# RWKV stage of a two-layer backbone: a new order of one body's work, a gather into two buffers, four spreads instead of eight, and y's stores on two queues

## The chip, the cores and the metric

The kernel runs on one core of a Trainium2 chip. The core has a matrix engine (TensorE, "PE" in the profile, its weight loads "PEld"), a vector engine (VectorE, "DVE"), a scalar engine (ScalarE, "ACT"), a general engine (GpSimd, "POOL") and SyncE ("SP"), which here only issues DMAs. Each engine runs its own list of instructions in order, and the engines meet through semaphores. The metric is the device time of one execution in microseconds, the median of the runs; lower is better.

## The reference

Two layers over a latent stream of 2048 tokens and a context of 256 tokens, width 1024. The first layer mixes with multi-head latent attention and a Fourier transform. The second is a bidirectional RWKV-7 time mix. Only its scan matters here:

```python
def step(s, inp):
    w_t, k_t, v_t, kk_t, a_t = inp[:5]
    sa = jnp.einsum('bhvk,bhk->bhv', s, kk_t)
    s = (s * w_t[:, :, None, :]
         - sa[..., None] * (kk_t * a_t)[:, :, None, :]
         + v_t[..., None] * k_t[:, :, None, :])
    y = jnp.einsum('bhvk,bhk->bhv', s, inp[5]) if len(inp) > 5 else None
    return s, y
```

There are 16 heads of width 64 and two directions; the state of a head is 64 x 64 and runs over all 2304 tokens. Both directions' y are added, normalised by head, gated and projected. Everything is float32.

## The kernel before

Stages follow each other: modulation, the first layer's projections, attention, Fourier mixing, merge, the second layer's input projection (`project1`), the scan (`rwkv`, L1663), and the last merge (`merge1`, L2433). The change touches only `rwkv`.

**Tiling.** Heads are worked in pairs (a pair fills 128 partitions), tokens in groups of 256, a group in 4 chunks of 64. 8 pairs times 9 groups give 72 bodies, each with both directions (d = 0 forward, d = 1 backward). The loop over bodies is unrolled (`bodies`, L1764).

**A chunk as matrices.** Inside a chunk the recurrence becomes a triangular system. For a chunk: products of keys with queries are made (`scores`, matmul L1972) and masked (`masks`, L2357) into tiles NB (removal) and KK (new keys). The 64 x 64 triangular part of NB is inverted: its 16 x 16 diagonal blocks on GpSimd (`invert`), the parts off the diagonal by three rounds of matmuls (`far_p` L1988, `first_order` L1998, `second_w` L2007, `higher_orders` L2017), whose sums VectorE adds (`add_orders`, rw_XT, L2376).

**The way of the blocks.** SP stores NB's blocks to `scratch_products` (`keep_products`, L1808), fetches the diagonal blocks into g_in and g_at (`gather`, L1816), GpSimd inverts them, SP stores g_out (`keep_inverses`, L1823) and fetches them spread over XB (`spread`, eight DMAs, L1834).

**The serial part.** For each chunk c of body n: `step_values` (L2026), `step_begin` (the read of the state S: L2036, and the start of the update and of y: L2043 to L2050), ScalarE copies r1 (`take_r1`, L2206), `step_sa` (L2062, needs XT), ScalarE copies sa (`take_sa`, L2210), `step_end` (L2070 into S's bank, L2075 into y's), VectorE writes the state (`carry`, L2349), ScalarE copies y (`take_y`, L2220). `step_begin` of the next chunk reads S, and after that read waits for `take_y`, since y's bank is written again. I call the four carries of a body c0 to c3.

**Work ahead.** Each body also does pieces for later bodies: m = n+1 (far blocks), k = n+3 (turns: transposes of K, B, V through TensorE, L1953, with four copies on ScalarE, L2196; scores, masks, the bonus L1936 and L2340), l = n+4 (low-rank L1928, rates L2163, decays L2177, keys, queries L2325, weights L2334 and L2335). Loads (L1780, L1781) are for n+5. The order of all this on each engine is written out by hand in a function `body(n, has)` for each engine; `has` drops the parts that fall off either end. y of the body before is stored by ScalarE in two pairs of DMAs (`store_y`, L2226).

A PSUM bank is shared by several of these: bank 5 holds scores of direction 0 and the bonus, bank 3 scores of direction 1 and the turned V, bank 4 the turned K and B in turn.

## Time and profile before

| | us |
|---|---|
| median of 3 runs (5325.24 to 5332.35) | 5329.45 |
| profiled execution | 5343.89 |
| its span, first to last instruction | 5341.9 |

| engine | busy us | share of the span | instructions |
|---|---|---|---|
| PE | 4732.2 | 89% | 50126 |
| DVE | 2522.5 | 47% | 4088 |
| ACT | 1828.2 | 34% | 4367 |
| POOL | 1306.7 | 24% | 2817 |

The span's shares mix stages with different limits: the RWKV stage is the part from about 3,600 to 5,060 us. A busy matmul engine is a modelled figure, since matmuls overlap. Rows give the engine, the line, the operation and tiles as out<-in; the bracket at a row's end is how long the engine stood idle before it, and who ended that.

### The profile page before, as it was taken

The page shows a single profiled execution, that of the slowest core. Times are in us where ns is not written, and L with a number is a line of the kernel's source. Part 1 is how long each engine was busy: PE and PEld are TensorE (multiplying, and loading weights), DVE is VectorE, ACT ScalarE, POOL GpSimd, SP SyncE. Part 2 cuts the span into 40 slices and gives each one's busy share as a digit, 9 for nine tenths or more (in the row PEclk, how much of TensorE's full clock was granted, in tenths as well). Part 3 has the DMA queues.
Part 4 walks back from the last instruction along what each step waited for, and adds up shares of the span by engine and source line. Part 5 has one row for each costly group of instructions (what it writes and reads, how often), then busy time and mean ns, then how long its engine had stood idle before and what let it go on. Part 6 is the DMA issues. An engine that isn't in the chain of part 4 may idle for free. (4 is left out here: it accounts for less than half of the span.)

```text
span 5341.9 us, 125176 instructions
## 1 busy us (share of the span) xinstructions
PE 4732.2 (89%) x50126; PEld 2658.0 (50%) x50126; DVE 2522.5 (47%) x4088; ACT 1828.2 (34%) x4367; POOL 1306.7 (24%) x2817
## 2 busy tenths in 40 slices
PE   5999996999999997898999999967888888888689
PEld 2666663333333333444444444436666666666544
DVE  1334433666666662222222222235666666666476
ACT  1221221443343431132211212125555555555322
POOL 0111111222222220000000000005655565565333
PEclk7999997999999998999999999989999999999899
DMA  7221211000000006432211112135666666666475
GB/s 290 61 64 62 70 61 63 4 23 24 23 23 22 23 6 245 163 137 60 73 59 59 59 59 71 55 90 133 149 151 142 145 149 138 150 147 144 106 267 172
DMA packets 928982, 526.66 MB, mean 99 GB/s; under 512 B 661344, under 2 KB 879072, under 8 KB 921440
## 3 DMA queue, kind: packets, MB, share of 16 engines
q1 hardware_dynamic: 850144, 500.73, 32.7%
q10 hardware_dynamic: 78336, 18.89, 1.7%
q8 instruction: 357, 5.85, 0.5%
q14 instruction: 145, 1.19, 0.1%
HBM read 330.98 MB, written 188.49 MB: 97 GB/s over the span
## 5 line engine op out<-in xcount | busy, mean ns | idle before, releaser
L1565 PE MATMUL p_bU<-keep_hT,p_slab 128*128 128x512 f32 (+1 forms) x2592 | 1029.5, 559 | 12.9 <-DMA p_slab<-in_o_w_in_dram 7.5
L1565 PEld LDWEIGHTS p_bU<-keep_hT,p_slab 128*128 128x128 f32 x2592 | 493.3, 191 | 544.1 <-issue 512.3
L914 PE MATMUL at_bS<-at_qT,at_kT 97*64 97x512 f32 (+1 forms) x2368 | 602.5, 598 | 6.7 <-issue 6.1
L1046 DVE TENSOR_REDUCE at_mx<-at_bM 128x1 f32<-128x512 f32 (+1 forms) x656 | 400.5, 629 | 355.3 <-PE at_bM L880 352.4
L1009 ACT ACTIVATE at_pT<-at_bS 128x512 f32<-128x512 f32 (+1 forms) x592 | 346.9, 591 | 461.4 <-PE at_bS L914 382.4
L1637 DVE SCALAR_TENSOR_TENSOR p_z<-p_u,p_shift,p_z 128x2306 f32<-128x2306 f32 x26 | 68.2, 2622 | 770.3 <-ACT p_z L1595 770.3
L1892 POOL TENSOR_TENSOR rw_g_at<-rw_g_at,rw_g_prod 64x14 f32<-64x14 f32 (+6 forms) x1008 | 318.0, 315 | 79.0
L1890 POOL TENSOR_TENSOR rw_g_prod<-rw_g_at 64x14 f32<-64x14 f32 (+6 forms) x1008 | 314.2, 312 | 79.1
L2349 DVE TENSOR_TENSOR rw_S<-rw_bank,rw_dec 128x128 f32<-128x128 f32 x288 | 84.1, 292 | 474.2 <-PE rw_bank L2070 474.2
L933 PE MATMUL at_bO<-at_pT,at_va 128*64 128x512 f32 x1152 | 300.3, 599 | 0.0
L837 POOL TENSOR_TENSOR at_sum_pool<-at_sum_pool,at_pT 128x512 f32<-128x512 f32 x128 | 192.8, 1506 | 433.3 <-ACT at_pT L1009 421.9
L914 PEld LDWEIGHTS at_bS<-at_qT,at_kT 97*64 97x64 f32 x2368 | 161.1, 138 | 266.2 <-issue 214.0
L1589 ACT COPY p_u<-p_bU 128x512 f32<-128x512 f32 (+1 forms) x130 | 69.7, 542 | 643.6 <-PE p_bU L1565 630.0
L1067 DVE TENSOR_TENSOR at_sum_vector<-at_sum_vector,at_pT 128x512 f32<-128x512 f32 x320 | 276.2, 863 | 13.1 <-ACT at_pT L1009 9.7
L1903 POOL MEMSET rw_zeros<- 128x1040 f32 x1 | 1.0, 964 | 1105.0 <-POOLq L2685 1105.0
L1355 PE MATMUL m_bY<-m_w,m_mT 128*128 128x512 f32 x576 | 251.8, 595 | 0.0
L453 PE MATMUL p_bG<-keep_w_in,p_hT 128*128 128x512 f32 x576 | 250.1, 592 | 0.0
L880 PE MATMUL at_bM<-at_kTb,at_qTb 96*64 96x512 bf16 (+1 forms) x1312 | 224.4, 365 | 12.0 <-DVE at_mx L1046 10.9
L2576 PE MATMUL m_bY<-m_w,m_oT 128*128 128x512 f32 x512 | 225.3, 599 | 1.5 <-DVE m_oT L2646 1.5
L2043 PE MATMUL rw_bank<-rw_Vt,rw_Kt 64*64 64x64 f32 x2304 | 183.8, 228 | 27.9 <-ACT rw_ysb L2220 19.5
L2062 PE MATMUL rw_bank<-rw_r,rw_XT 64*64 64x64 f32 x2304 | 133.3, 233 | 79.8 <-DVE rw_XT L2376 74.8
L1972 PE MATMUL rw_bank<-rw_AR,rw_Kc 64*64 64x128 f32 x2304 | 168.1, 279 | 37.4 <-issue 30.1
(263 smaller groups left out, 9401.7 us busy)
## 6 DMA issues: line engine op xcount, KB each, us to landing
rw_zin<-scratch_heads SPq DMA_DIRECT2D x144, 512.0 KB, 4.9
rw_XB<-scratch_inverses SPq DMA_DIRECT2D x576, 64.0 KB
mod_w<-in_ada_w_dram SPq DMA_DIRECT2D x6, 4096.0 KB, 23.6
scratch_heads<-p_z SPq DMA_DIRECT2D x24, 1024.0 KB, 4.9
rw_lin<-scratch_lora SPq DMA_DIRECT2D x144, 128.0 KB, 5.5
scratch_bv<-rw_bv SPq DMA_DIRECT2D x144, 128.0 KB, 2.3
scratch_products<-rw_NB SPq DMA_DIRECT2D x288, 64.0 KB, 3.9
scratch_y<-rw_ysb ACTq DMA_DIRECT2D x288, 64.0 KB, 2.8
```

What stands on the lines that cost most here:

```text
L453: last = pe.matmul(bG[:, j, :], hT[:, s, k, :], w_in[:, k, E_G0 + 512 * j:E_G0 + 512 * (j + 1)], start=(k == 0), stop=(k == KD - 1))
L880: last = pe.matmul(bM[rows, (FIRST_ITEM[b] + i) % 2, 0:n], qTb[:, s, q0 + VH * x:q0 + VH * x + VH], kTb[:, s, c:c + n], start=True, stop=True)
L914: last = pe.matmul(bS[rows, g % 3, 0:nq * P], kT[:, s, k * P + VH * x:k * P + VH * x + VH], qT[:, s, q0 * P:(q0 + nq) * P], start=True, st ...
L933: last = pe.matmul(out[rows, 0:nq * P], va[:, s, 2 * pair + x, :], pT[:, (g + x) % SLOTS, 0:nq * P], start=(pair == 0), stop=(pair == nk / ...
L1009: nc.scalar.activation(pT[:, g % SLOTS, 0:n], bS[:, g % 3, 0:n], ACT.Exp, scale=SCALE).then_inc(exp_done, 1)
L1046: nc.vector.tensor_reduce(mx[:, j, piece:piece + 1], bM[:, (FIRST_ITEM[b] + i) % 2, 0:n], AX.X, ALU.max).then_inc(max_red, 1)
L1067: nc.vector.tensor_tensor(acc, acc, tile, ALU.add).then_inc(added[False], 1)
L1355: last = pe.matmul(bY[:, j, :], mT[:, s, k, :], w[:, k, j * 512:(j + 1) * 512], start=(k == 0), stop=(k == KD - 1))
L1565: last = pe.matmul(bU[:, n % 4, 0:w], slab[:, i, k, :], hT[:, k, tok:tok + w], start=(k == 0), stop=(k == KD - 1))
L1890: link(nc.gpsimd.tensor_tensor(prod, N[:, k + 1:, k:k + 1].broadcast_to([2 * half, rows, k]), N[:, k:k + 1, 0:k].broadcast_to([2 * half, r ...
L1892: link(nc.gpsimd.tensor_tensor(below, below, prod, ALU.add))
L2576: last = pe.matmul(bY[:, 2 * s + j, :], oT[:, s, k, :], w[:, k, j * 512:(j + 1) * 512], start=(k == 0), stop=(k == KD - 1))
```

## The change

Bodies compute the same. Parts:

- Blocks: g_in and g_at get two buffers each, and both receive all 64 diagonal blocks. The layout in the scratch tensors is changed so that each spread fetches both directions at once, four DMAs in place of eight; `crossed` and `laid` keep the books. `gather` waits for the inversion two bodies back, no longer for the last one.
- GpSimd: two turned copies at the start instead of one reversed, and two copies out over 64 partitions instead of four over 32.
- SP's order in a body: y's store of direction 1, spread, products, bonus store, loads, gather, inverses. Before: bonus store, loads, products, inverses, gather, spread.
- TensorE: scores of direction 0 come right behind the first step's begin; the bonus and the turns of V and B come behind chunk 1's begin; the scores of L1972 against Kc for direction 1 move to chunk 3.
- ScalarE: y's store of direction 0 behind the copy of sa; the copies of turned tiles move one or two chunks later, half of the turned K into the next body.
- VectorE: queries behind carry 2, the bonus product behind carry 1, its queries for k = n+3 behind carry 0.

```diff
-        g_in, g_at = (core.sb(n, [2 * BLOCKS, SUB * SUB]) for n in ("g_in", "g_at"))
+        g_in, g_at = (core.sb(n, [2 * BLOCKS, 2, SUB * SUB]) for n in ("g_in", "g_at"))
...
                 def gather(m):
                     sp.wait_ge(n_st, 16 * 4 * (m.n + 1))
-                    if m.since(1):
-                        sp.wait_ge(inv_done, 4 * m.n)
-                    for d in range(2):
-                        sp.dma_start(by_block((g_in, g_at)[d], d), diagonal("products")[BLOCKS * d:BLOCKS * (d + 1)]).then_inc(g_l, 16)
+                    if m.since(2):
+                        sp.wait_ge(inv_done, 2 * m.n - 2)
+                    for tile in (g_in, g_at):
+                        sp.dma_start(by_block(tile[:, m.two]), diagonal("products")).then_inc(g_l, 16)
...
-                    for turned in (1, 0):
-                        for d in range(2):
-                            for h, (rows, other) in enumerate(ACROSS):
-                                sp.dma_start(XB[rows if turned else other, m.two, turned, d], whole("inverses", d, h, turned)).then_inc(xb_l, 16)
+                    for order in range(2):
+                        for half, (rows, _) in enumerate(HEADS2):
+                            sp.dma_start(XB[rows, m.two, order].rearrange("p d c t -> p (d c) t"), delivered(order, half)).then_inc(xb_l, 16)
...
                 def body(n, has):                        # SP
+                    if has[0] and n.since(1):
+                        store_y(n.on(-1), 1)
+                    if has[1]:
+                        spread(n.on(1))
                     if has[3]:
+                        keep_products(n.on(3))
                         store_bonus(n.on(3))
                     if has[5] and n.since(-3):
                         load(n.on(5))
                     if has[3]:
-                        keep_products(n.on(3))
+                        gather(n.on(3))
                     if has[2]:
                         keep_inverses(n.on(2))
-                    if has[3]:
-                        gather(n.on(3))
-                    if has[2]:
-                        spread(n.on(2))
...
                 def body(n, has):                        # TensorE, first half
-                    if has[3]:
-                        bonus(k)
                     if has[0]:
                         step_values(n, 0, lambda i: higher_orders(n, 0, (2 * i, 2 * i + 1)))
                         step_begin(n, 0, lambda i: higher_orders(n, 1, (2 * i, 2 * i + 1)))
                     if has[3]:
-                        turn(k, 2)
+                        scores_free(k, 0, 0)
+                        scores(k, 0, 0, range(NCH))
...
+                    if has[3]:
+                        bonus(k)
                     if has[0]:
                         step_sa(n, 1)
                     if has[3]:
-                        scores(k, 0, 1, (2, 3))
+                        turn(k, 2)
                     if has[0]:
                         step_end(n, 1)
+                    if has[3]:
+                        turn(k, 1)
...
                 def body(n, has):                        # ScalarE
                     if has[0]:
                         take_r1(n, 0)
+                    if has[2]:
+                        for e in range(2):
+                            turned(j, 0, 1, e)
+                    if has[0]:
+                        take_sa(n, 0)
                         if n.since(1):
                             store_y(n.on(-1), 0)
                     if has[3]:
-                        for h in range(2):
-                            for e in range(2):
-                                turned(k, 2, h, e)
                         decay_of_chunks(k)
-                    if has[0]:
-                        take_sa(n, 0)
...
                     if has[0]:
                         take_y(n, 0)
                         take_r1(n, 1)
-                        if n.since(1):
-                            store_y(n.on(-1), 1)
```

ScalarE around a body's first step, before (rw_r is r1, rw_ee the rates, rw_Vt the turned V):

```order
L2206 COPY rw_r<-rw_bank 128x128
L2226 DMA scratch_y<-rw_ysb 64x4x64 x2
L2196 COPY rw_Vt<-rw_bank 64x4x64 x4
L2185 COPY rw_dec<-rw_ep 128x4
L2186 COPY rw_dec<-rw_ep 128x4
L2210 COPY rw_sa<-rw_bank 128x128
L2163 ACTIVATE rw_ee<-rw_bank,rw_par 128x256 x2
L2220 COPY rw_ysb<-rw_bank 128x2x64
L2206 COPY rw_r<-rw_bank 128x128
```

The same place after, from the end of one body into the next:

```order
L2210 COPY rw_Kt<-rw_bank 64x4x64 x2
L2220 COPY rw_r<-rw_bank 128x128
L2210 COPY rw_Kt<-rw_bank 64x4x64 x2
L2224 COPY rw_sa<-rw_bank 128x128
L2240 DMA scratch_y<-rw_ysb 64x4x64 x2
L2199 COPY rw_dec<-rw_ep 128x4
L2200 COPY rw_dec<-rw_ep 128x4
L2177 ACTIVATE rw_ee<-rw_bank,rw_par 128x256 x2
L2234 COPY rw_ysb<-rw_bank 128x2x64
L2220 COPY rw_r<-rw_bank 128x128
```

The copy of sa moved ahead of the store of y, the decay copies stay behind the store, and the copy of y (rw_ysb) now has the store in front of it.

VectorE from the last carry of a body to the first of the next, before:

```order
L2349 TENSOR_TENSOR rw_S<-rw_bank,rw_dec 128x128
L2334 TENSOR_TENSOR rw_Kc<-rw_kd,rw_en 128x512
L2335 SCALAR_TENSOR_TENSOR rw_Bc<-rw_b,rw_en 128x512
L2325 TENSOR_TENSOR rw_AR<-rw_ep,rw_zin 128x8x64
L2326 TENSOR_TENSOR rw_AR<-rw_ep,rw_zin 128x8x64
L2340 TENSOR_TENSOR rw_bv<-rw_bank,rw_zin 128x512
L2376 TENSOR_TENSOR rw_XT<-rw_bank,rw_XT 128x256 x2
L2349 TENSOR_TENSOR rw_S<-rw_bank,rw_dec 128x128
```

And after:

```order
L2366 TENSOR_TENSOR rw_S<-rw_bank,rw_dec 128x128
L2351 TENSOR_TENSOR rw_Kc<-rw_kd,rw_en 128x512
L2352 SCALAR_TENSOR_TENSOR rw_Bc<-rw_b,rw_en 128x512
L2393 TENSOR_TENSOR rw_XT<-rw_bank,rw_XT 128x256 x2
L2374 TENSOR_TENSOR rw_NB<-rw_bank,rw_tri 128x512
L2366 TENSOR_TENSOR rw_S<-rw_bank,rw_dec 128x128
```

Three operations left the stretch ahead of rw_XT, and one mask came in behind it.

SP over one body, before, from the bonus store:

```order
L1789 DMA scratch_bv<-rw_bv 128x256 x2
L1780 DMA rw_zin<-scratch_heads 128x4x256
L1781 DMA rw_lin<-scratch_lora 64x2x256
L1780 DMA rw_zin<-scratch_heads 128x4x256
L1781 DMA rw_lin<-scratch_lora 64x2x256
L1808 DMA scratch_products<-rw_NB 64x4x64 x4
L1823 DMA scratch_inverses<-rw_g_out 128x16x16
L1816 DMA rw_g_in<-scratch_products 32x16x16
L1816 DMA rw_g_at<-scratch_products 32x16x16
L1834 DMA rw_XB<-scratch_inverses 64x4x64 x8
```

And after, from the store of y:

```order
L1851 DMA scratch_y<-rw_ysb 64x4x64 x2
L1845 DMA rw_XB<-scratch_inverses 64x8x64 x4
L1820 DMA scratch_products<-rw_NB 64x4x64 x4
L1797 DMA scratch_bv<-rw_bv 128x256 x2
L1788 DMA rw_zin<-scratch_heads 128x4x256
L1789 DMA rw_lin<-scratch_lora 64x2x256
L1788 DMA rw_zin<-scratch_heads 128x4x256
L1789 DMA rw_lin<-scratch_lora 64x2x256
L1828 DMA rw_g_in<-scratch_products 64x16x16
L1828 DMA rw_g_at<-scratch_products 64x16x16
L1835 DMA scratch_inverses<-rw_g_out 128x16x16
```

Products moved ahead of the bonus store and the loads; the gather moved behind the loads and has twice the rows; the spread stands at the body's start.

## Rows read from the trace of the kernel before

**Rows 1.** One stretch: busy us of PE, PEld, DVE, ACT, POOL; clock, DMA share, GB/s.

```profile
4000.00:4400.00 400.00, 326.62 (x10226) 269.51 (x10223) 252.39 (x504) 234.36 (x703) 230.53 (x686) 0.97 0.64 146
```

**Rows 2.** The carry's line: duration ns min/median/max, first and last start us.

```profile
L2349 DVE TENSOR_TENSOR rw_S<-rw_bank,rw_dec x288: 291/292/293, 3638.4 to 5055.2; 128x128 f32<-128x128 f32 x144
```

**Rows 3.** Timeline: carries of one body and TensorE's issue wait (start us, us).

```profile
4235.97 0.29 DVE L2349 TENSOR_TENSOR rw_S<-rw_bank,rw_dec 128x128 f32<-128x128 f32 x1 [2.09 <-PE rw_bank L2070]
...
4239.71 0.29 DVE L2349 TENSOR_TENSOR rw_S<-rw_bank,rw_dec 128x128 f32<-128x128 f32 x1 [0.99 <-PE rw_bank L2070]
...
4243.14 0.29 DVE L2349 TENSOR_TENSOR rw_S<-rw_bank,rw_dec 128x128 f32<-128x128 f32 x1 [0.61 <-PE rw_bank L2070]
...
4244.21 0.45 PE L1998 MATMUL rw_bank<-rw_XB,rw_Pm 64*64 64x64 f32 x8 [0.61 <-issue]
...
4247.63 0.29 DVE L2349 TENSOR_TENSOR rw_S<-rw_bank,rw_dec 128x128 f32<-128x128 f32 x1 [1.08 <-PE rw_bank L2070]
...
4253.85 0.29 DVE L2349 TENSOR_TENSOR rw_S<-rw_bank,rw_dec 128x128 f32<-128x128 f32 x1 [2.05 <-PE rw_bank L2070]
```

**Rows 4.** Waits of TensorE, 3,800 to 4,880 us: total us, times, longest.

```profile
PE rw_bank L2062 <- DVE rw_XT L2376: 56.4, 52, 1.3
PE rw_bank L2070 <- ACT rw_sa L2210: 37.6, 68, 1.8
PE rw_bank L1998 <- issue: 23.7, 13, 3.3
PE rw_bank L2043 <- ACT rw_ysb L2220: 12.8, 23, 0.6
```

**Rows 5.** Timeline of VectorE, from a body's c3 to the next c0.

```profile
4208.45 0.29 DVE L2349 TENSOR_TENSOR rw_S<-rw_bank,rw_dec 128x128 f32<-128x128 f32 x1 [1.04 <-PE rw_bank L2070]
...
4209.86 0.69 DVE L2325 TENSOR_TENSOR rw_AR<-rw_ep,rw_zin 128x512 f32<-128x512 f32 x1
...
4211.88 0.74 DVE L2376 TENSOR_TENSOR rw_XT<-rw_bank,rw_XT 128x256 f32<-128x256 f32 x2
```

**Rows 6.** Timeline of TensorE, the same stretch.

```profile
4208.32 1.12 PE L1936 MATMUL rw_bank<-rw_q,rw_same 128*128 128x512 f32 x2
...
4210.94 0.66 PE L1953 MATMUL rw_bank<-keep_ident,rw_zin 128*128 128x128 f32 x4
4212.76 0.45 PE L2062 MATMUL rw_bank<-rw_r,rw_XT 64*64 64x64 f32 x8 [1.17 <-DVE rw_XT L2376]
4213.01 1.09 PE L1928 MATMUL rw_bank<-rw_lin,rw_wl 64*64 64x256 f32 x16
4214.32 0.27 PE L2070 MATMUL rw_bank<-rw_sa,rw_Bt 64*64 64x64 f32 x2 [0.21 <-ACT rw_sa L2210]
```

**Rows 7.** Timeline of ScalarE; ACTq is its DMA issue.

```profile
4210.22 1.84 ACTq L2226 DMA_DIRECT2D scratch_y<-rw_ysb  x2
4212.15 1.50 ACT L2196 COPY rw_Vt<-rw_bank 64x256 f32<-64x256 f32 x4 [1.67 <-PE rw_bank L1953]
...
4214.16 0.85 ACT L2163 ACTIVATE rw_ee<-rw_bank,rw_par 128x256 f32<-128x256 f32 x2
...
4216.11 1.27 ACTq L2226 DMA_DIRECT2D scratch_y<-rw_ysb  x2
```

**Rows 8.** SP: issues of one body, and its longest wait in 54 bodies.

```profile
4208.48 5.59 SPq L1834 DMA_DIRECT2D rw_XB<-scratch_inverses  x8
...
SPq L1816 <- DMA scratch_products<-rw_NB: 82.9, 51, 3.3
```

**Rows 9.** Waits of GpSimd, the same 54 bodies.

```profile
POOL rw_g_at L1884 <- DMA rw_g_at<-scratch_products: 310.6, 54, 9.7
```

**Rows 10.** DMA: busy tenths (40 slices) from 4,217.4 to 4,223.4; then packets 4,209.4 to 4,229.4.

```profile
DMA  6689999999999798999899999999999999987653
...
DMA packets 9474, 2.96 MB, mean 148 GB/s; under 512 B 7934, under 2 KB 9470, under 8 KB 9470
...
q8 instruction: 4, 0.07, 1.4%
```

More of the change, by code:

```diff
@@ L1742, in rwkv, with crossed, laid @@
         ACROSS = [(HEADS2[h][0], HEADS2[1 - h][0]) for h in range(2)]
+        def crossed(h, d):
+            return h if d == 0 else 1 - h
+        def laid(turned, d):
+            return 1 - turned if d == 0 else turned
         def pos(d, c):
@@ L1987, in far_p @@
                         for rows, other in ACROSS:
-                            last = pe.matmul(bank[INV_AT[d]][other, C * c:C * c + C], NB_[rows, m.kept, d, c, 0, :], XB[rows, m.two, 1, d, c, :],
+                            last = pe.matmul(bank[INV_AT[d]][other, C * c:C * c + C], NB_[rows, m.kept, d, c, 0, :], XB[rows, m.two, laid(1, d), d, c, :],
                                              start=(c == 0), stop=True, skip_group_check=True)
@@ L1997, in first_order @@
                         for rows, _ in HEADS2:
-                            last = pe.matmul(bank[INV_AT[d]][rows, GT + C * c:GT + C * c + C], Pm[rows, d, c, :], XB[rows, m.two, 0, d, c, :],
+                            last = pe.matmul(bank[INV_AT[d]][rows, GT + C * c:GT + C * c + C], Pm[rows, d, c, :], XB[rows, m.two, laid(0, d), d, c, :],
                                              start=(c == 0), stop=True, skip_group_check=True)
@@ L2141, in body @@
                         step_values(n, 3)
-                        step_begin(n, 3)
+                    if has[3]:
+                        scores_free(k, 1, 1)
+                        scores(k, 1, 1, (0, 1))
+                    if has[0]:
+                        step_begin(n, 3, (lambda i: scores(k, 1, 1, (2 + i,))) if has[3] else None)
+                    elif has[3]:
+                        scores(k, 1, 1, (2, 3))
                     if has[3]:
@@ L2262, in body @@
                     if has[3]:
-                        turned(k, 1, 0, 1)
+                        turned(k, 2, 0, 1)
+                        for e in range(2):
+                            turned(k, 2, 1, e)
                     if has[0]:
                         take_sa(n, 2)
-                    if has[3]:
-                        for e in range(2):
-                            turned(k, 1, 1, e)
                     if has[4]:
@@ L2272, in body @@
                         take_y(n, 2)
+                    if has[3]:
+                        turned(k, 1, 0, 0)
+                    if has[0]:
                         take_r1(n, 3)
+                    if has[3]:
+                        turned(k, 1, 0, 1)
+                        for e in range(2):
+                            turned(k, 1, 1, e)
+                    if has[0]:
                         take_sa(n, 3)
@@ L2374, in add_orders @@
                     grown = XT[:, m.two, d].rearrange("p c t -> p (c t)")
-                    less = grown if which else XB[:, m.two, 0, d].rearrange("p c t -> p (c t)")
+                    less = grown if which else XB[:, m.two, laid(0, d), d].rearrange("p c t -> p (c t)")
                     nc.vector.tensor_tensor(grown, bank[INV_AT[d]][:, XT_COLS], less, ALU.add).then_inc(xt_out[d], 1)
@@ L2389, in body @@
                     link = Link(v, dch, EL * l.n)
-                    if has[3]:
-                        bonus(k)
                     if has[0]:
```

144 lines of the change are left out of this document (69 added, 75 removed).

## The prediction, made before the changed kernel ran

> **What bounds the kernel now.** I read the busy times by stretch first. The RWKV stage runs from about 3,600 us to 5,055 us, and in it no engine is full: in 400 us TensorE is busy 327, VectorE 252, ScalarE 234, GpSimd 231, the DMA engines 64%, at a granted clock of 0.97 of the full 2.4 GHz [rows 1]. So the stage is bound by the order in which engines wait for each other. Its clock is the carry of the state, four times a body: 288 carries from 3638.4 to 5055.2 us, thus 1416.8 / 71.75 = 19.75 us a body [rows 2]. Next I read single carries, to know a body when little disturbs it. c0 to c0 takes 3.74 + 3.43 + 4.49 + 6.22 = 17.88 us in one body [rows 3]; the average body is 1.87 us longer. The waits of TensorE, over 54 bodies, name two kinds of loss [rows 4]. One is order: 56.4 us for rw_XT (1.04 a body), 37.6 for rw_sa (0.70), 12.8 for rw_ysb. The other is called "issue": the sequencer waits for nothing that the profile shows. The largest issue group has 23.7 us in 13 waits, the longest 3.3 us. I read these as code that arrives late: four packets of a queue of kind "instruction" land in 20 us, 0.07 MB together, while loads of the next body fill the DMA engines for over 5 us on end [rows 10].
>
> The inversion on GpSimd does not bound it. It sits idle 310.6 us in 54 bodies, 5.75 a body, for its gathered blocks [rows 9], so a loop of 14 us of work has room in 19.75.
>
> **The change, part by part.** Times of one body, c3 at 4208.45 us.
>
> *From c3 to c0.* Before, the bonus matmul (1.12 us, until 9.44) stood ahead of the new body's first work [rows 6], and the values' matmuls (0.25) ahead of the read of S, near 9.7. It goes; the read can start when the carry is written (8.45 + 0.29 and a hand-over), so about 0.9 earlier. Then VectorE: Kc, Bc, two AR from 9.86, bv, then XT at 11.88, done at 12.62; TensorE waited 1.17 us for it and began the sa matmul at 12.76 [rows 5, 6]. After, only Kc and Bc stand ahead of XT, to 9.86, and the matmuls that XT adds up, which end where the turn begins (10.94), end 0.9 earlier, so XT is ready near 10.75. In the place of the turn of V (4 records in 0.66 us) stand all scores of one direction, 16 records of 128 columns. Bound below by half of the low-rank's 16 records of 256 columns (1.09 / 2 = 0.55), above by 1.09; I take 0.8, nearer to the middle because records have a start that does not halve. sa then starts at 10.9, low-rank takes 1.09 behind it, and the update of the state starts at 12.25 instead of 14.32. ScalarE hides: its copy of sa no longer stands behind y's store, four turned copies (1.50 us) and two of the decay, only behind two turned copies. Gain 2.05 us.
>
> *From c0 to c1.* Here a new wait appears. ScalarE's store of y (two DMAs, 1.27 us in one place and 1.84 in the other, during which it does nothing else [rows 7]) moves behind the copy of sa, together with the decay copies (0.3) and two rates (0.85), and only then comes the copy of y (0.27), which frees the bank that TensorE writes next. sa's copy ends at about 11.7; 11.7 + 1.27 + 0.3 + 0.85 + 0.27 = 14.4, while TensorE comes at 13.4 (carry at 12.8, its read 0.35 later, 0.2 of matmuls). So 1.0 us of waiting (1.6 if the store takes 1.84). Queued behind it: the rest of the step, the bonus matmul (1.06 more here), sa, the turn of V, and by them the next carry. Rest 0.7, bonus 1.06, sa 0.25, its copy 0.55, carry 0.5 give c1 at 17.5, 4.7 after c0, against 3.73. Loss 0.95. The other store of y, on SP's queue now, costs ScalarE nothing; that saves a second 1.27, which lay beside TensorE's work except for some 0.3 of waiting for sa.
>
> *From c1 to c2.* The turn of B comes ahead of the values and the far products behind the start of the step instead of in front. The same work stands in both, but the scores that filled TensorE's wait for the copy of sa are gone. Bounds: nothing, or 0.5 (a copy of 0.27 and two hand-overs). I take 0.2 loss.
>
> *From c2 to c3.* The turn of K must wait until ScalarE has copied all of the turned B. Three of those copies (1.50 for four [rows 7], so 1.1) now stand behind the copy of r1, beside which TensorE has only half a microsecond of the step left. Bounds: 0.6 later, if the copies hide behind a full step, to 1.3 with the 0.2 of scores in front of the step. The stretch in rows 3 (4.49) has an issue wait of 0.61 in it [rows 3], which a body without stalls has not, so against it the loss is between 0 and 0.7. I take 0.6, since the copies stand right behind r1.
>
> *SP's queue and GpSimd.* Eight spreads took 5.59 us to issue [rows 8]; four take 2.8, or 5.6 if twice the rows cost twice the issue; both fit ahead of the far products. SP waited 82.9 us in all for products to land before it could gather [rows 8]; now loads and bonus stores fill that time. All of this is hidden already: TensorE's waits have no group for rw_XB worth a term, so it earns 0. It must not become late, though. Products issued 3 us into the body land by 8 or so, the gather goes out behind the loads near 15, lands by 20, the inversion takes 14, its store 3, and the spread goes out at a body's start and lands some 5 us in; the far products ask for it near 9. That leaves 3 to 4 us. The gathered blocks are fetched twice (64 KB instead of 32 for each tile): 1,024 more packets in 9,474 a body [rows 10]. The inverter's four copies out of 32 partitions become two of 64: less work, on an idle engine, 0.
>
> The Trainium skill, "DMA: Bandwidth & Descriptors", section Specifications, asks for at least 512 B a descriptor, and the doubled gather moves 64 B pieces; by that it would be the dearest part. The trace has DMA engines 64% busy with most packets under 512 B already, so it decides little here.
>
> *Sum.* 17.88 - 2.05 + 0.95 + 0.2 + 0.6 = 17.6 us for a body without stalls. The order alone thus gives 0.3 against the quick body. The rest hangs on code stalls. Before, they and what hangs on them are 19.75 - 17.88 + 0.6 = 2.5 us a body. After, TensorE stands 1.0 and 1.0 us still at two new places in the quick half of a body, and code can arrive meanwhile. Bounds: none is absorbed (2.5) or both waits swallow their like (0.5). I take 1.5. Body: 19.1, or 0.6 to 0.65 less; times 72 is 43 to 47. The profiled execution took 5343.9 us with a span of 5341.9; the median of the runs is 5329.45, 14.4 less, and I take the gain from that: 5286.
>
> **Rivals.**
> *No gain.* Stalls only move: with 2.2 a body, 19.8 again, 5320 to 5339. For it: the stalls stand at several lines [rows 4], so their place hardly matters. Against it: the quick body lost only 0.6 to them, while single waits elsewhere reach 3.3 [rows 3, 4], so they depend on what runs beside them.
> *Slower.* Loads now go out behind the bonus store, and that behind c1: their saturated 5 to 8 us cover the far products, both last steps and the second-order matmuls, where TensorE runs through code fastest. Two of four code packets are then late instead of one. Price: stalls of 3.3 instead of 2.5, so 17.6 + 3.3 = 20.9 at worst, 20.6 at 3.0; 0.85 times 72 is 61: 5390. It decides from 2.2 of stalls a body. For it: saturation before began already at c1 [rows 10], and moving it later by 3 us keeps it in the quick half. Against it: products no longer stand behind the loads.
> *Large gain.* Nearly all stalls fall under the two waits: 17.6 + 0.8 = 18.4, 1.35 times 72 is 97: 5232.
> *Blocks late.* If the spread misses the far products, body length is set by GpSimd's 14 us plus a hand-over of 5, 19 us: the forecast's time by another way, so it needs no chance of its own.
>
> **How the numbers follow.** Forecast 0.50, no gain 0.14, slower 0.20, large gain 0.16. Two tenths of a percent is 10.7 us, about what a measurement of this kernel can tell from no change: below 5319 is faster, above 5340 slower. Faster 0.67 (forecast, large gain, a little of no gain), same 0.12, slower 0.21. The forecast's own range is 5262 to 5310; the whole range is 5222 to 5352.
>
> **What would show it.** TensorE's group of rw_XT under the sa matmul falls from 56.4 us to under 15; that of rw_ysb rises from 12.8 to over 40; a new group for the turn of K behind ScalarE's rw_Bt appears with 30 to 60; c3 to c0 falls to near 4.3 us, c0 to c1 rises to 4.7. Issue waits, all groups, fall by a third. GpSimd's wait stays 4 us a body or more. It is wrong if a group for rw_XB shows on TensorE, if low-rank waits for the loads, or if issue waits grow.

## The result: 0.6% slower, and where the time went

The changed kernel takes 5358.0 us (median of 5 runs, 5350.2 to 5368.6), the kernel before 5329.2 (5 runs, 5325.2 to 5332.4). The ratio is 1.0059, 95% interval 1.0046 to 1.0072. The forecast was 5286 us. The profiled execution took 5368.6 us with a span of 5366.8; before it was 5343.9 and 5341.9, so the two profiles differ by 25 us where the medians differ by 29.

The profile of before is thus of an execution 14.7 us above its median, or 0.2 us a body; where bodies of two profiles are compared below, a difference of that size can be chance.

First the same stretch of 400 us as [rows 1] (busy us of PE, PEld, DVE, ACT, POOL; clock, DMA share, GB/s):

```profile
4000.00:4400.00 400.00, 333.72 (x10114) 278.02 (x10106) 250.56 (x496) 223.16 (x694) 236.82 (x649) 0.98 0.70 147
```

TensorE ran fewer matmuls in it (10,114 for 10,226) and was busy longer; the DMA engines went from 64% to 70%. The carry's line answers to [rows 2]; duration in ns, then first and last start:

```profile
L2366 DVE TENSOR_TENSOR rw_S<-rw_bank,rw_dec x288: 258/292/293, 3640.6 to 5080.8; 128x128 f32<-128x128 f32 x144
```

(5080.8 - 3640.6) / 71.75 = 20.07 us a body, for 19.75 before: 0.33 more, times 72 is 24 us, the whole difference of the two profiles. So nothing outside of this stage is needed to explain it.

The timeline of VectorE gives one body, as [rows 3] do (start, us, and in brackets the idle time before and its releaser):

```profile
4319.97 0.29 DVE L2366 TENSOR_TENSOR rw_S<-rw_bank,rw_dec 128x128 f32<-128x128 f32 x1 [2.05 <-PE rw_bank L2087]
...
4323.31 0.71 DVE L2323 TENSOR_TENSOR_SCAN rw_cs<-rw_reset,rw_ee 128x256 f32<-128x256 f32 x1
4324.05 0.29 DVE L2366 TENSOR_TENSOR rw_S<-rw_bank,rw_dec 128x128 f32<-128x128 f32 x1
...
4328.38 0.75 DVE L2381 TENSOR_TENSOR rw_Pm<-rw_bank,rw_far 128x256 f32<-128x256 f32 x2
4329.04 0.28 DVE L2366 TENSOR_TENSOR rw_S<-rw_bank,rw_dec 128x128 f32<-128x128 f32 x1
...
4334.12 0.29 DVE L2366 TENSOR_TENSOR rw_S<-rw_bank,rw_dec 128x128 f32<-128x128 f32 x1 [2.04 <-PE rw_bank L2087]
...
4339.52 0.29 DVE L2366 TENSOR_TENSOR rw_S<-rw_bank,rw_dec 128x128 f32<-128x128 f32 x1 [1.31 <-PE rw_bank L2087]
```

c0 to c1 is 4.08, c1 to c2 4.99, c2 to c3 5.08, c3 to c0 5.40. The second and the third of these carries, c1 and c2, have no bracket: VectorE came to them straight from the instruction before. That is so at 66 of the 72 carries c1 and 69 of the 72 carries c2; before, it was so at none, and in [rows 3] all five had waited for TensorE. Only c2 pays for it. The last matmuls into S's bank ahead of these two carries:

```profile
4323.78 0.23 PE L2087 MATMUL rw_bank<-rw_sa,rw_Bt 64*64 64x64 f32 x2
...
4328.45 0.23 PE L2087 MATMUL rw_bank<-rw_sa,rw_Bt 64*64 64x64 f32 x2
```

c1 starts 0.04 us behind their end, c2 0.36. Over the stage the medians are 0.05 and 0.37 us after, 0.05 and 0.12 before.

The starts of all 288 carries, read from that timeline, give each of the four stretches over the stage (a quickest tenth is the tenth percentile of each stretch by itself):

```
us                       c0-c1   c1-c2   c2-c3   c3-c0   body
before, mean              3.96    4.59    4.99    6.23   19.75
after, mean               4.98    4.23    5.14    5.73   20.07
before, quickest tenth    3.73    3.43    4.08    5.97
after, quickest tenth     4.07    4.04    5.08    4.56
forecast, no stalls       4.68    3.63    5.09    4.17   17.6
```

The waits of TensorE, 3,820 to 4,900 us, hence 53.8 bodies, answer to [rows 4] (total us, times, longest):

```profile
PE rw_bank L1968 <- ACT rw_Bt L2210: 38.9, 51, 0.8
PE rw_bank L2060 <- ACT rw_ysb L2234: 32.0, 36, 2.1
PE rw_bank L2034 <- issue: 22.3, 12, 3.4
PE rw_bank L2087 <- ACT rw_sa L2224: 19.7, 53, 0.4
```

An "issue" wait is idle time of TensorE that nothing in the profile ends. The rw_XT group is gone; the turn of K waits for the turned B, and rw_ysb rose from 12.8 to 32.0, not to over 40. All groups of that view together, by the body: issue 1.62 before and 1.53 after, waits for engines or transfers 1.96 and 1.81. So the listed waits fell a little. What is left of a body, busy time and gaps too short for the view, grew from 16.17 to 16.73, more than the body itself. Issue waits did not fall by a third, but they moved. By the TensorE timeline of the whole stage 1.46 of 1.52 us a body stood between c1 and c3 before; now 1.15 of 1.42 stand between c3 and c0.

Issue waits above 0.3 us end some 2.8 us (tenth to ninetieth percentile 2.3 to 3.3, 84 waits) behind the start of a packet of 16 KB of the queue of kind "instruction"; before it was 2.5 us (2.3 to 2.8, 81 waits). There are four such packets a body in both kernels. That ties most of these waits to code that arrives late, and suggests that it came 0.3 us slower. It is a reading of times that go together; "late code" below means these waits.

The DMA engines show why it may. First 6 us around a c3 (4,312.3 to 4,318.3, c3 at 4314.26; 40 slices), then the queue SP issues to, over 3,820 to 4,900 us (packets, MB, share of 16 engines), in the kernel after:

```profile
DMA  9999977879999999999999999985646100158788
...
q1 hardware_dynamic: 506679, 146.86, 64.7%
```

and the same queue in the kernel before:

```profile
q1 hardware_dynamic: 435341, 139.39, 55.9%
```

In [rows 10] the full stretch lay from c1 (4218.6) to c2 (4222.0); now it ends behind c3. On average over the bodies, counting packets where they start (a value above 1 means that they run on into the next us):

```
us after c3          0    1    2    3 ...  10   11   12   13   14   15   16   17   18   19
DMA share before  0.29 0.32 0.36 0.71     0.95 0.99 0.96 0.94 0.80 0.70 0.64 0.54 0.42 0.28
DMA share after   0.84 0.82 0.62 0.60     0.61 0.47 0.43 0.52 0.50 0.71 0.83 0.90 1.04 1.13
64 B before        146   62    9    7        0    0    0   29  197  504  694  695  515  222
64 B after         555  892  765  566        0    0    0    0    0    0    0    3  187  514
```

Before, the 64 B packets (gathers and the inverses' store) ran behind the loads. Now there are 3,967 a body instead of 2,982, and they run into the loads: the trace's packets of 64 B take 13 ns of a DMA engine on average, for 10 before, which makes 3.12 us of all 16 engines a body for 1.92. The median is 11 ns in both, so a part of the packets take much longer.

Two issuing engines feel it too. ScalarE and SP, in their timelines (ACTq and SPq are DMA issues):

```profile
4613.39 2.34 ACTq L2240 DMA_DIRECT2D scratch_y<-rw_ysb  x2
4615.82 0.20 ACT L2199 COPY rw_dec<-rw_ep 128x4 f32<-128x4 f32 x1 [2.17 <-issue]
```

```profile
4331.23 0.57 SPq L1828 DMA_DIRECT2D rw_g_in<-scratch_products  x1
4331.85 0.81 SPq L1828 DMA_DIRECT2D rw_g_at<-scratch_products  x1
4332.76 4.05 SPq L1835 DMA_DIRECT2D scratch_inverses<-rw_g_out  x1
```

The store of y, 1.3 us on ScalarE in most bodies, takes 2.3 in some, and y's copy, for which TensorE waits, stands behind it. The issue of the inverses' store had a median of 383 ns (72 issues) and has 2,880 now, behind loads and gathers. GpSimd still has room ([rows 9]: 310.6 us in 54 bodies), so the inversion is not the bound:

```profile
POOL rw_g_at L1906 <- DMA rw_g_at<-scratch_products: 317.4, 53, 9.9
```

### The profile page after: what moved, and what is told of

The parts are those of the page before. It is cut to its first block and busy times, and to the rows that moved or that the text cites. A ratio compares the mean times of both kernels' runs of the same rounds, so it can differ in the third digit from the quotient of the medians.

```text
span 5366.8 us, 124754 instructions
## 1 busy us (share of the span) xinstructions
PE 4770.7 (89%) x50126; PEld 2696.2 (50%) x50126; DVE 2531.2 (47%) x4088; ACT 1801.9 (34%) x4367; POOL 1328.2 (25%) x2745
## 5 line engine op out<-in xcount | busy, mean ns | idle before, releaser
L1565 PE MATMUL p_bU<-keep_hT,p_slab 128*128 128x512 f32 (+1 forms) x2592 | 1029.4, 559 | 12.8 <-DMA p_slab<-in_o_w_in_dram 7.3
L1914 POOL TENSOR_TENSOR rw_g_at<-rw_g_at,rw_g_prod 64x14 f32<-64x14 f32 (+6 forms) x1008 | 344.9, 342 | 79.0
L1912 POOL TENSOR_TENSOR rw_g_prod<-rw_g_at 64x14 f32<-64x14 f32 (+6 forms) x1008 | 335.1, 332 | 79.1
L1989 PE MATMUL rw_bank<-rw_AR,rw_Bc 64*64 64x128 f32 x2304 | 197.7, 288 | 21.9 <-issue 12.6
L2224 ACT COPY rw_sa<-rw_bank 128x128 f32<-128x128 f32 x288 | 76.7, 266 | 404.8 <-PE rw_bank L2079 404.8
L404 POOL TENSOR_TENSOR p_hr<-p_hms,p_half 128x8 f32<-128x8 f32 x36 | 58.9, 1637 | 576.5 <-DVE p_hms L589 576.5
```

The source lines that it names most:

```text
L1565: last = pe.matmul(bU[:, n % 4, 0:w], slab[:, i, k, :], hT[:, k, tok:tok + w], start=(k == 0), stop=(k == KD - 1))
L1912: link(nc.gpsimd.tensor_tensor(prod, N[:, k + 1:, k:k + 1].broadcast_to([2 * BLOCKS, rows, k]), N[:, k:k + 1, 0:k].broadcast_to([2 * BLOCK ...
L1914: link(nc.gpsimd.tensor_tensor(below, below, prod, ALU.add))
```

## Experiments

Ratios are against the kernel before, run on the same chip, with the 95% interval. "Body" is the span of the 288 carries / 71.75, and waits are by the body over 3,820 to 4,900 us, both in the one profiled execution of each kernel, which lay up to 15 us from its median. The expectations number their theories: 1, the place of the loads; 2, the doubled gathers; 3, ScalarE's store of y.

**The two halves of the change, and the store of y.** The change was split into its order and its transfers.

```
order_only: engines' order of after; transfers of before
  sp: store_y(n-1,1) keep_products(n+3) store_bonus(n+3) load(n+5) keep_inverses(n+2) gather(n+3) spread(n+2)
transfers_only: engines' order of before; two block buffers, doubled gathers, four spreads
  sp: spread(n+1) store_bonus(n+3) load(n+5) keep_products(n+3) gather(n+3) keep_inverses(n+2)
y_on_sp:
-  scalar: store_y(n.on(-1), 0)
+  sp:     for d in range(2): store_y(n.on(-1), d)
```

> The changed kernel with the transfers of before: half gathers into one buffer, eight spreads at a body's end, the four copies of the inverter. The order of TensorE, ScalarE and VectorE and y's store on SP are the changed ones. Theory 1 (the order puts the loads, and the code that arrives beside them, under c3 to c0, where no wait takes the stall in): this kernel loses as the changed one does, 5345 to 5365 us, TensorE's issue waits stay 1.2 to 1.6 us a body with two thirds of them in c3 to c0. Theory 2 (the doubled gathers fill the DMA engines and make code and stores late): the forecast's gain comes out here, under 5320.

Measured: 5491.9 us, 1.0308 (1.0294 to 1.0321), body 21.68. Neither theory: TensorE's waits have a group that neither kernel had.

```profile
PE rw_bank L1997 <- issue: 50.2, 36, 3.2
PE rw_bank L1937 <- DMA rw_lin<-scratch_lora: 42.5, 26, 3.9
```

The low-rank matmuls wait for the loads. SP's queue stands at a body's end for the inverses (90.9 us in 50 bodies, two groups) ahead of the next body's products, bonus store and loads. It stood as long before (103.1 us in 55 bodies), but there the bonus store and the loads came first in a body and did not wait for the bonus of a later chunk. That the new order needs the new queue order is argued from this and no run shows it; the run puts no price on the order.

> The kernel before with the new transfers alone: blocks gathered whole into two buffers, four spreads at a body's start, two inverter copies; every engine's order, and SP's bonus store and loads ahead of the products, as before. Theory 1 (order and the place of the loads): within 0.2% of before, 5320 to 5340. Theory 2 (doubled gathers): 0.3 to 0.6% slower, 5345 to 5362, with issue waits of TensorE above 1.5 us a body.

Measured: 5357.6 us, 1.0051 (1.0037 to 1.0065), body 20.09. The time is theory 2's, the reason is not, since issue waits are down to 1.1 us a body:

```profile
PE rw_bank L2076 <- DVE rw_XT L2390: 61.4, 53, 1.8
PE rw_bank L1986 <- DMA rw_XB<-scratch_inverses: 34.8, 24, 4.5
```

The spread at a body's start, behind SP's wait for the inverses to land (190.8 us), is late for this order. So it is no clean measure of the transfers; spreads_alone and before_double are. In the profile 0.6 us a body of new wait stand beside 0.5 less of late code.

> The changed kernel with both stores of y on SP's queue, so that ScalarE issues no transfer in the stage. Theory 3 (ScalarE's store, 1.1 to 2.6 us, holds the copy of y and with it TensorE in c0 to c1): the wait for rw_ysb, 0.61 us a body, goes, c0 to c1 falls from 4.98 to 4.3, 5310 to 5320. Theory 1 alone (what waits took in comes back as stalls): issue waits rise by as much as the y wait falls, 5345 to 5360. If SP's queue becomes the limit, a wait for rw_XB shows up on TensorE and the time goes above 5370.

Measured: 5354.3 us, 1.0048 (1.0035 to 1.0061); against after a gain of about 0.1%, within the intervals. The rw_ysb group is gone from TensorE (0.59 us a body) and c0 to c1 fell to 4.41, but issue waits rose from 1.53 to 1.87 and c1 to c2 from 4.23 to 4.57. The time is theory 1's; of the 0.59 us of wait 0.34 are seen to come back as late code.

**Light loads.**

```
-  sp.dma_start(zin[:, s, d], src)
+  sp.dma_start(zin[:, s, d, 0:1], src[:, 0:1])      # loads in the bodies only
```

> The changed kernel, but each body's load brings one of the four input fields instead of four (128 KB instead of 512 for each direction); the rest is left as it lies, so what is computed is not the reference's. Theory 1 (stalls and long issues come from loads that fill the DMA engines): issue waits of TensorE fall from 1.4 to under 0.5 us a body, c3 to c0 from 5.7 to 4.4, ScalarE's store stays near 1.1 us; body 18.3, so 5358 - 72 x 1.8 = 5228. Rival (code comes late whatever else the engines carry, since TensorE runs through it faster than it is brought): issue waits stay above 1.1 a body and the time above 5300.

Measured: 5282.5 us, 0.9907 (0.9892 to 0.9923), body 18.95. Issue waits are 0.54 us a body, c3 to c0 4.79 (expected under 0.5 and 4.4). The gain is 75 us where 130 were expected, so the loads are not all of it. The rival, that code is late whatever else runs, is out.

> The kernel before with each body's load cut to one of the four input fields, as light_after has it; what is computed is not the reference's. light_after took 5282.5 us, 0.9907 of before, with a body of 18.95 us. Theory 1 (the change loses since its c3 to c0 and c0 to c1 now lie under loads): without the loads' weight the change wins as its order promised, by 0.2 to 0.3 us a body, so light_before takes 5295 to 5310. Rival (stalls and waits swallow each other wherever the loads are): the old order has more waits to hide code behind and profits as much from light loads: within 0.2% of light_after, or faster, 5260 to 5290.

Measured: 5292.7 us, 0.9922 (0.9897 to 0.9947), body 19.06. Under theory 1's range and within 0.2% of light_after, as the rival had it. Issue waits are 0.23 us a body, and now a single buffer and its late spread show:

```profile
PE rw_bank L2062 <- DVE rw_XT L2376: 56.3, 56, 1.4
PE rw_bank L1972 <- DMA rw_XB<-scratch_inverses: 41.7, 24, 2.7
```

So even without the weight of the loads the change is worth 0.1 us a body, which the intervals do not tell from nothing, and not 0.3. And the old order loses 0.7 us a body here to the late blocks alone, which the change cures; by that count the rest of the new order gains nothing.

**The doubled gathers.** This part was priced at nothing.

```
half_gather:   -  for tile in (g_in, g_at): all 64 rows
               +  g_in rows 0:16, g_at 16:32, g_in 32:48, g_at 48:64   (four DMAs)
four_gathers:  +  rows 0:32 and 32:64 of both tiles                    (four DMAs, all rows)
before_double: before, with both gathers of all 64 rows
spreads_alone: before, with two buffers, half gathers, four spreads; SP's old order, spread last
transfers_half: transfers_only with half gathers
```

> The changed kernel, with each gather bringing only the half of the blocks that its tile uses (four DMAs of 16 rows instead of two of 64 rows; 1,024 packets of 64 B fewer a body). Theory 2 (the doubled gathers weigh on the DMA engines beside the end of the loads, and make code late under c3 to c0): DMA share falls from 0.69 to 0.66, issue waits from 1.5 to 1.1 us a body, 5325 to 5340. Theory 1 (place of the loads, not the gathers): within 0.2%, 5348 to 5368.

Measured: 5322.3 us, 0.9988 (0.9976 to 1.0001), body 19.45: 0.7% under after. Issue waits are 1.09 a body, c3 to c0 fell from 5.73 to 5.15, the other three stretches changed by 0.15 at most.

```profile
DMA packets 499457, 159.58 MB, mean 148 GB/s; under 512 B 413158, under 2 KB 499174, under 8 KB 499174
...
q1 hardware_dynamic: 469383, 148.28, 62.3%
```

> The changed kernel with its doubled gathers cut into four DMAs of 32 rows: all 2,048 blocks are still fetched twice over, only the number of DMAs is that of half_gather. If packets are what costs: as the changed kernel, 5350 to 5370, 64 B packets near 3,970 a body and c3 to c0 near 5.7. If it is the size of one DMA (small ones land earlier): as half_gather, 5315 to 5335.

Measured: 5353.2 us, 1.0048 (1.0033 to 1.0062), body 19.94. The packets cost, not the size of a DMA: half_gather and this one have the same number of DMAs and lie 0.6% apart, with intervals that do not touch. Some 0.1% may come from the smaller DMAs. But two details of the account do not hold here: c3 to c0 is 5.34 and not near 5.7, with 1.27 us of issue waits, and the 64 B packets take 11.1 ns, though there are as many and they start in the same places. So neither the ns of a packet nor c3 to c0 alone carries the cost.

> The kernel before with one change: both gathers bring the rows of all blocks, as the changed kernel's do (64 KB instead of 32 each, 1,024 packets of 64 B more a body); one buffer, eight spreads and every order as before. Theory 2 (the doubled gather itself costs, since its small packets run beside loads and code; half_gather against the changed kernel gave 36 us): 0.3 to 0.7% slower, 5345 to 5370, with DMA share up by 0.03 to 0.05 and 64 B packets at more than 10 ns each. Theory 1 (it costs only where the changed order has the gather beside c3 to c0): within 0.2%.

Measured: 5343.1 us, 1.0031 (1.0021 to 1.0041), body 19.80. The same packets cost 17 us in the old kernel, half of the 31 to 36 that they cost in the new one. There their 64 B packets take 10 ns; they run when the loads are through.

> The kernel before with two block buffers, half gathers, two inverter copies and four spreads, SP's queue in its old order (spread last). Theory: these parts are free, as nothing on TensorE waits for them: within 0.2% of before, 5315 to 5335, a wait for rw_XB under 5 us in 54 bodies. Rival (128 KB spreads or the inverter's two copies from one tile cost by themselves): above 5345, as transfers_half (5381).

Measured: 5329.7 us, 0.9992 (0.9981 to 1.0002). The spreads, the second buffer and the inverter's two copies are free, as forecast. The kernel's rw_XB wait is 0.7 us in 55 bodies.

> transfers_only with half gathers: the kernel before with two block buffers, four spreads at a body's start and two inverter copies. transfers_only took 5357.6 us and its TensorE waited 34.8 us in 54 bodies for rw_XB, which before did only for 1.8. Theory 2 (the doubled gather makes all of its loss): 5320 to 5335, the rw_XB wait under 15. Rival (the spread at a body's start, behind SP's wait for the inverses, is late for the old order's early far products, doubled or not): 5340 to 5358, the rw_XB wait over 25.

Measured: 5380.9 us, 1.0099 (1.0083 to 1.0114), against 1.0051 with doubled gathers. The rival had said that the loss stays; that it grows by half a per cent with fewer packets neither theory gives, and it is the opposite of half_gather. The rw_XB wait is the same (36.1), issue waits are 1.41 a body for 1.12. This stays open. What the run does show, beside spreads_alone, is the price of SP's order: with the same transfers, the spread at a body's start instead of its end costs the old order 51 us.

**The place of the loads.**

```
late_heads (rw_lin gets a semaphore of its own, for low_rank):
-  sp: ... load(n+5)       gather(n+3) keep_inverses(n+2)
+  sp: ... load_rates(n+5) gather(n+3) keep_inverses(n+2) load_heads(n+5)
late_heads_y_sp: and both stores of y on SP.  half_late_y: and half gathers
```

> The changed kernel, but SP issues the 1 MB of input fields (rw_zin) behind the gather and the inverses' store, with a semaphore of its own for the small low-rank input, which stays where it was. The saturated stretch moves from before c3 into the next c0 to c1. Theory 1: c3 to c0 falls from 5.73 to below 5.0, its issue waits from 1.15 to under 0.6; part of it comes back in c0 to c1, where ScalarE's store grows longer beside loads: net 5320 to 5345. Rival (stalls fall wherever TensorE runs through code fastest, whatever the loads do): c3 to c0 keeps 5.5 or more and the time is 5350 to 5370.

Measured: 5337.1 us, 1.0008 (0.9996 to 1.0020), body 19.49, c3 to c0 5.31, issue waits 1.30 a body: 0.5% under after, inside theory 1's 5320 to 5345. But c3 to c0 is not below 5.0, its issue waits are 0.9 and not under 0.6, and the theory's reason doesn't hold as it was put. 6 us around a c3 (4304.2; from 2 us before it):

```profile
DMA  9510000797888887769559999999997789999999
```

The loads fill the engines from c3 on (share 0.85 to 0.99 in each of the first seven us after it), under the very stretch that got shorter. What changed is that the 64 B packets no longer run beside them: they come 14 to 20 us after c3, at a share of 0.5 to 0.8, and take 11 ns for 13. So loads under c3 to c0 don't hurt by themselves; loads and small packets together do, as the pairs of runs further down bear out.

> late_heads with both stores of y on SP's queue. With the wait for rw_ysb gone and the loads under c0 to c1: if the two gains add (0.3 and 0.3 to 0.5 us a body), 5300 to 5325, better than before. If a wait removed only comes back as late code, as between the changed kernel and y_on_sp (wait -0.6, issue +0.3 a body), 5335 to 5355.

Measured: 5315.0 us, 0.9962 (0.9948 to 0.9976), body 19.56 in the profile. Faster than both kernels. The store of y moved to SP is worth 0.5% here, and was worth 0.1% in the changed kernel.

> The changed kernel with all three edits: half gathers, the input fields loaded behind the inverses' store, both stores of y on SP. Singly they gave 36, 21 and 4 us, the last two together 43. If they add: 5275 to 5290. If they work by one cause, fewer filled DMA engines beside code, the later ones find less to take away: 5290 to 5310. Issue waits 1.2 to 1.5 us a body, since no y wait takes them in.

Measured: 5302.5 us, 0.9957 (0.9941 to 0.9973), body 19.16: no measurable gain over late_heads_y_sp. With the loads apart, 1,024 packets more cost next to nothing. That is the second expectation, of edits that work by one cause.

**Is a wait worth its length?** One copy moved on ScalarE, in four surroundings, and one step more.

```
-  take_y(n, 2)  turned(k, 1, 0, 0)  take_r1(n, 3)  turned(k, 1, 0, 1)
+  take_y(n, 2)  turned(k, 1, 0, 0)  turned(k, 1, 0, 1)  take_r1(n, 3)
..._fill: TensorE's scores(k, 1, 0, (3,)) behind step_sa(n, 2); VectorE's masks(k, 1, 0) behind carry(n, 2)
```

> half_late_y with the second copy of the turned B ahead of the copy of r1 of step 3 instead of behind it. It runs in time in which ScalarE waits for r1 (0.96 us a body in the changed kernel). The wait of the turn of K for the turned B, 0.7 us a body, halves. If the order's waits are worth their length: c2 to c3 falls from 5.08 to 4.7 and the time by 20 to 27 us against half_late_y. If code that is late takes it back: c2 to c3 falls likewise but c3 to c0 grows, and the time falls by under 10 us.

Measured: 5274.4 us, 0.9899 (0.9884 to 0.9914), body 18.95. 28 us for 0.36 us of wait a body:

```profile
PE rw_bank L2101 <- ACT rw_sa L2238: 20.8, 56, 0.4
PE rw_bank L1982 <- ACT rw_Bt L2224: 18.9, 50, 0.4
```

> The changed kernel with the second turned B ahead of r1's copy in step 3, nothing else. In half_late_y that edit took 28 us (5302.5 to 5274.4). If a wait is worth its length whatever the DMA engines carry: 5328 to 5338 here too. If with the doubled gathers the time that it frees is filled by late code in c3 to c0: c2 to c3 falls to 4.7, c3 to c0 rises above 5.8, 5343 to 5358.

Measured: 5353.6 us, 1.0052 (1.0037 to 1.0068), for 1.0059. c2 to c3 fell from 5.08 to 4.70 (quickest tenth), c3 to c0 rose to 5.82. The second branch by its time: nearly all of it is taken back. By what, the profile doesn't say: issue waits are 1.49 us a body for 1.53.

> half_gather (0.9988 of before) with the second turned B ahead of r1's copy. If the doubled gathers beside c3 to c0 were what turned the freed time into late code: the edit is worth 20 to 27 us here, ratio 0.994 to 0.995. If it needs the loads out of c3 to c0 (theory 1): under 10 us, ratio 0.997 to 0.999.

Measured: 5325.7 us, 0.9984 (0.9974 to 0.9995), for 0.9988. Taken back too: c3 to c0 5.15 to 5.47, issue waits 1.09 to 1.36. So the doubled gathers are not what eats it.

> late_heads_y_sp (0.9962 of before), whose gathers are doubled, with the same edit. If the place of the loads decides: 20 to 27 us, ratio 0.991 to 0.993. If the doubled gathers decide: under 10 us, ratio 0.994 to 0.996.

Measured: 5287.9 us, 0.9907 (0.9892 to 0.9923), for 0.9962. Worth 0.55% here, with doubled gathers: it is the moved loads and stores. Which of the two wasn't tried.

The runs now hold six pairs that differ only in the gathers:

| surroundings | doubled | half |
|---|---|---|
| changed kernel | 1.0059 | 0.9988 |
| the same, copy moved | 1.0052 | 0.9984 |
| input fields late, y on SP | 0.9962 | 0.9957 |
| the same, copy moved | 0.9907 | 0.9899 |
| kernel before | 1.0031 | 1 |
| transfers_only | 1.0051 | 1.0099 |

The doubling costs twice 0.7%, twice 0.1% or less, once 0.3%, and once it gains half a per cent; each measured ratio has some 0.15% either way.

> half_late_y_turned, with the far products one chunk ahead of the K scores, the last of these scores in the wait for the copy of sa in step 2, and VectorE's mask of them behind carry 2 instead of ahead. VectorE came to carry 2 without any idle time in the changed kernel, and TensorE waited 0.37 us a body for sa there. If both go: c1 to c2 falls from 4.05 to 3.6 and the time by 20 to 30 us, 5245 to 5255. If late code takes it: c1 to c2 has quick bodies of 3.6 but issue waits rise, 5265 to 5280.

Measured: 5270.8 us, 0.9896 (0.9879 to 0.9913). The quickest quarter of c1 to c2 fell from 4.05 to 3.72, so VectorE's mask had indeed held carry 2; the mean only from 4.58 to 4.25, c0 to c1 rose from 4.78 to 5.03 and issue waits from 1.46 to 1.60. No measurable gain: the second branch. This is the end of that road; it and half_late_y_turned are 1.0% faster than the kernel before and 1.6% faster than the changed one.

## Why the prediction was wrong

*The order's sum held, its terms less.* 17.6 us without stalls were forecast; the quickest twentieth of each stretch sums to 17.35 in after and to 17.17 in light_after. But by the same measure the kernel before has 17.00, and light_before 16.93. The sum said so too: it took 17.6 against a "quick body" of 17.88, but that body holds an issue wait of 0.61, as its own stall term grants, and 17.27 is left. The order thus costs 0.3 us a body and gains nothing, and the whole forecast gain hung on the stalls falling from 2.5 to 1.5. c3 to c0: forecast 4.17, quick 4.2 to 4.6. c2 to c3: forecast 5.09, measured 5.08, with the new wait of the turn of K at 38.9 us (30 to 60 foretold). c0 to c1: 4.68 with a y wait of 1.0 in every body; it is 4.07 in the quick tenth and 5.01 in the median, with 0.59 us of y wait a body, so the mechanism is right and its size depends on how long the store's issue takes. c1 to c2: "I take 0.2 loss" was 0.6, 4.05 for 3.43, and in nearly every body. That term had only TensorE in it. VectorE now has bv, two keys, a mask and the blocks between carry 1 and carry 2 and comes to carry 2 without a pause, 0.37 us behind TensorE; the fill experiment gave 0.33 back.

*The doubled gather was the first failed step.* "The trace has DMA engines 64% busy with most packets under 512 B already, so it decides little here", and the sum took 0. Measured by half_gather against after it is 0.7%, by four_gathers against half_gather 0.6%: 31 to 36 us, more than the whole loss of 29. The order and all other parts together then come to 0.9988 of before (0.9976 to 1.0001), a gain of 7 us that is not clear of noise, where 43 were forecast. Of the 72 us between forecast and measurement the gather is nearly half. The Trainium skill, "DMA: Bandwidth & Descriptors", section Specifications, had been cited against it with its 512 B a descriptor and waved off by the average share. The runs agree with the page in direction, and show what it does not: the price went with what the packets met. It was 31 to 36 us beside the loads, 17 behind them in the old kernel, and too little to measure once the input fields and y's stores were moved. The issue of the inverses' store shows the meeting by itself: a median of 2.88 us in after, 0.40 in half_gather, 0.61 in light_after and in late_heads. How the packets lengthen a body is not shown, and transfers_half contradicts the sign.

*"I take 1.5" of stalls was the second, and the rest of the miss.* Beyond the quick body after loses 2.5 us, just the bound "none is absorbed"; with half gathers 1.85 (19.45 - 17.6) are left. The idea behind it was right in part: less wait went with more late code in y_on_sp and half_turned, and more wait with less in transfers_only, though not in turned_alone. But the two new waits stand in c0 to c1 and c2 to c3, and code came late in c3 to c0, from which the change had taken the 1.0 us of waiting for XT. That this removed the cover at the place where loads and small packets now met is the reading that fits; no run put the wait back.

*The rivals and the signs.* "Slower" named the right start, loads behind the bonus store, and that under c1; and the right kind of loss. It had no small packets in it and put the loss behind c1, while it stands behind c3. Its 5390 was too dear: it wanted stalls of 3.0, 2.5 came. "No gain" gave 5320 to 5339, too fast. "Code is late whatever the order is", the reason that spoke for "No gain", does not hold: with light loads and the same packets of code the issue waits fell to 0.54 and 0.23 us a body. "Blocks late" was right in that it didn't decide. None of the three signs of being wrong showed: TensorE has no rw_XB group worth a term, low-rank waits 2.2 us in 54 bodies for its inputs, and issue waits did not grow. What had been promised and did not come is c3 to c0 near 4.3 (5.73), issue waits down by a third, and 40 us of waits for rw_ysb. The inverter was to have less work; GpSimd's busy time rose from 1306.7 to 1328.2 us, and nothing waited for it.

*Not settled.* Why transfers_half is slower than transfers_only. TensorE's rest of a body, busy time and gaps too short to be listed, is 16.0 to 16.4 us in the kernels with the old order and 16.4 to 16.8 with the new (order_only, at a clock of 0.94, 17.3). Some of it is longer matmuls (low-rank 386 to 410 ns a record, the scores of B 276 to 285, as the lines group them). That is the 0.3 us of the order and somewhat more, and no run took it apart. That late code is behind every issue wait rests on the packets' times and on the light loads; no run changed the amount of code.

## What to carry to other kernels

A transfer of small pieces has no fixed price: look at what fills the DMA engines when it runs, in the slices and not in the average share, and ask of every reordering which transfers it makes meet. Before a wait is taken away, look at whether it covers something, code that arrives late above all; the same copy moved was worth 0.5% in two kernels here and nothing in two others. And when a body's order is changed, walk every engine's queue up to the clocking instruction: here VectorE stood in front of a carry that only TensorE had been priced for. A quick body taken from the trace is a base for a sum only when its own stalls are taken out of it first, on both sides.

## What the hardware showed that had not been expected

- How long a DMA's issue blocks its engine depends on what was issued ahead of it: the same store of 128 KB had a median of 0.38 us before, 2.88 in after with a longest of 4.93, 0.61 with a quarter of the input fields, and 0.40 with half gathers. ScalarE's two y stores took 1.3 to 2.3 us.
- Packets of 64 B took 10 to 11 ns of a DMA engine on average when they ran apart from the loads, 11 to 13 when they ran into them; packets of 1,024 B 56 ns, and 53 with the loads apart.
- Three quarters less of the input fields took issue waits from 1.62 to 0.23 us a body in the old order and from 1.53 to 0.54 in the new, with the same four packets of code a body.
